# Moving the gate halves of tile 0 forward between the attention heads of a decoder block

## What is computed

```python
h = _modulate(x, sh1, sc1)
z = h @ w_in[l]
q, k, v, gu, gv, ga, gg = jnp.split(z, IN_SPLITS, axis=-1)
attn = _moba_attention(q.reshape(hs), k.reshape(hs), v.reshape(hs))
sgu = _chunked_sgu(gu, gv, sgu_ln_g[l], sgu_ln_b[l], w_spatial[l], b_spatial[l])
merged = (jax.nn.sigmoid(ga) * (attn @ w_attn_up[l])
          + jax.nn.sigmoid(gg) * (sgu @ w_gmlp_up[l]))
out = merged @ w_out[l]
```

## Time and profile before

| what | value |
|---|---|
| time, median of 3 runs | 951.78 us (950.54 to 952.5) |
| the profiled execution: its time | 948.68 us |
| the profiled execution: its span, first to last instruction | 946.9 us |
| PE matmul, busy | 782.7 us, 83% |
| DVE, busy | 605.0 us, 64% |
| ACT, busy | 192.6 us, 20% |
| POOL, busy | 537.0 us, 57% |
| transfers | 340.61 MB, 360 GB/s over the span |
| mean granted clock of PE | 0.923 of full speed |

### The profile page before, as it was taken

How to read it: one execution, slowest core, us unless ns; L and a number is a source line. 1 busy time by engine, 2 the same in 40 slices (tenths; PEclk the granted TensorE clock), 3 DMA queues, 4 the chain that set the end, 5 groups by cost and what they waited for, 6 DMA issues and landing times.

```text
span 946.9 us, 8889 instructions
## 1 busy us (share of the span) xinstructions
PE 782.7 (83%) x2974; PEld 464.0 (49%) x2974; DVE 605.0 (64%) x1359; ACT 192.6 (20%) x485; POOL 537.0 (57%) x529
## 2 busy tenths in 40 slices
PE   5989989999989867786969797797979769596964
PEld 5875568969944423442525353353534335252421
DVE  6356773244586538777674858567585858748556
ACT  1011033202031202231321212132121213312111
POOL 1000000001877776777777777777777777777772
PEclk9999979999999987988979898998989899797988
DMA  9999993323999999999999999999999999999994
GB/s 348 370 371 374 385 384 132 142 81 114 315 402 381 395 397 410 373 371 360 399 409 409 409 409 407 410 408 407 409 403 406 409 409 398 353 404 410 409 410 197
DMA packets 113356, 340.61 MB, mean 360 GB/s; under 512 B 9232, under 2 KB 21024, under 8 KB 113184
## 3 DMA queue, kind: packets, MB, share of 16 engines
q0 software_dynamic: 73728, 268.47, 72.3%
q1 hardware_dynamic: 37008, 69.21, 20.1%
q10 hardware_dynamic: 2576, 2.37, 0.8%
HBM read 338.96 MB, written 1.05 MB: 359 GB/s over the span
## 4 chain that ended last, share of the span: by engine, by line
POOL 35%; PE 29%; DMA 15%; issue 11%; DVE 8%; ACT 1%; SPq 0%; DVEq 0%; POOLq 0%
POOL ring L385 35%; PE bank L1212 13%; DMA ring<-in_w_cond_dram 8%; PE bank L1038 6%; DMA ring<-in_peer_u_dram,small 5%; DVE ln L646 4%; PE bank L1165 3%; PE bank L1187 2%; DMA wpq<-in_w_peer_q_dram 2%; PE bank L1126 2%; PE bank L1135 2%; DVE ring L868 1%; DVE ln L641 0%; PE bank L1087 0%; ACT small L554 0%
## 5 line engine op out<-in xcount | busy, mean ns | idle before, releaser
L1212 PE MATMUL bank<-ring,small 128*128 128x512 f32 x1012 | 474.7, 627 | 134.1 <-ACT small L554 134.1
L868 DVE CUSTOM_DVE_ANT_0 ring<-ring,h_sb 128x1024 f32<-128x1024 f32 x256 | 312.2, 1225 | 190.0 <-DMA ring<-in_peer_u_dram,small 182.7
L385 POOL DMA_INDIRECT ring<-in_peer_u_dram,small x256 | 264.4, 1033 | 263.6 <-DVE small L849 185.8
L1212 PEld LDWEIGHTS bank<-ring,small 128*128 128x128 f32 x1012 | 200.5, 202 | 388.3 <-issue 384.1
L385 POOL DMA_INDIRECT ring<-in_peer_v_dram,small x256 | 268.7, 1050 | 86.0 <-issue 72.9
L554 ACT ACTIVATE small<-ident,small 128x128 f32<-128x128 f32 x253 | 77.3, 388 | 48.4 <-DVE small L861 48.1
L544 ACT ACTIVATE small<-small 128x8 f32<-128x8 f32 x32 | 6.7, 210 | 378.4 <-DVE small L868 378.4
L1187 PEld LDWEIGHTS bank<-hT,wpq 128*128 128x128 f32 x512 | 59.4, 192 | 8.6 <-issue 6.2
L1187 PE MATMUL bank<-hT,wpq 128*128 128x128 f32 x512 | 60.0, 275 | 1.3 <-ACT hT L455 1.2
L646 DVE SCALAR_TENSOR_TENSOR ln<-ring,c_col,ln 128x512 f32<-128x512 f32 x77 | 57.9, 752 | 2.7
L1038 PEld LDWEIGHTS bank<-hT,ring 128*128 128x128 f32 x384 | 46.2, 201 | 2.8 <-issue 2.8
(11 more groups left out here) (158 smaller groups left out, 553.7 us busy)
## 6 DMA issues: line engine op xcount, KB each, us to landing
ring<-in_w_cond_dram SPq DMA_DIRECT2D x10, 2048.0 KB, 11.4
ring<-in_w_in_dram SPq DMA_DIRECT2D x8, 2048.0 KB, 15.2
wpq<-in_w_peer_q_dram SPq DMA_DIRECT2D x8, 1024.0 KB, 19.1
ring<-in_w_cond_dram SPq DMA_DIRECT2D x4, 1024.0 KB, 14.5
wpq<-in_w_out_dram SPq DMA_DIRECT2D x2, 2048.0 KB, 11.6
ring<-in_peer_u_dram,small POOLq DMA_INDIRECT x256, 6.7
ring<-in_peer_v_dram,small POOLq DMA_INDIRECT x256, 6.6
ring<-in_w_in_dram SPq DMA_DIRECT2D x2, 1024.0 KB, 13.5
```

What stands on the lines that cost most here:

```text
L385: nc.gpsimd.indirect_dma_start(out=dst[e], out_offset=None, in_=table[0], in_offset=bass.IndirectOffsetOnAxis(ap=idx[:, k:k + 1], axis=0)) ...
L868: V.tensor_tensor_reduce(u_ring[e], u_ring[e], h_sb[:, n // (2 * HEADS), :], 1.0, 0.0, ALU.mult, ALU.add, acol[:, n % 2, e:e + 1]).then_in ...
L1212: last = T.matmul(bank[ACC_BANKS[t][m]][:], diag[:, e, :], v_ring[e][:, m * BLK:(m + 1) * BLK], start=first, stop=end, skip_group_check=True)
```

## The change

A table says which halves stand behind which head's scores: 0, 1 and 2 behind head 0, half 3 behind head 1, none behind heads 2 and 3, and halves 4 to 7 behind heads 4 to 7 as before. On ACT the saves of halves 0 and 1 move ahead of the square root, the save of half 2 stands behind the exponentials of head 0, and that of half 3 behind those of head 1. Blank lines at the head of the file are dropped too, so the line numbers of the changed program are lower by 17 at ACT's first lines and by 14 on PE.

```diff
+HALVES = ((0, 1, 2), (3,), (), (), (4,), (5,), (6,), (7,))
...
                 if n == 5:
                     for m in range(2, 6):
                         save_wT(m)
+            save_half(0)
+            save_half(1)
             act.wait_ge(gvar_ready, 1)
             nc.scalar.activation(gst[:, 2, :], gst[:, 1, :], ACT.Sqrt, bias=eps[:], scale=1.0 / HD).then_inc(gstd_ready, 1)
...
                                              accum_out=asum[:, 0, j, t:t + 1]).then_inc(exp_done, 1)
-                    save_half(j)
+                    for i in HALVES[j][2 if j == 0 else 0:]:
+                        save_half(i)
...
             for j in range(HEADS + 2):
                 if j < HEADS:
                     scores(j)
-                    gate_half(j)
+                    for i in HALVES[j]:
+                        gate_half(i)
                 if j == 1:
                     cond_total(11)
```

## The result

The changed kernel takes 946.86 us (median of 15 runs, 944.22 to 951.86), the kernel before, beside it, 953.04 us (15 runs, 948.01 to 957.59). The ratio is 0.9944 with a 95% interval of 0.9919 to 0.9968, which on 952 us is 5.3 us less, between 3.0 and 7.7. Forecast were 945.5 us, a range of 943.4 to 949.2, and a gain of 6.3. Most of the 1.4 us between 945.5 and 946.86 is the base: the forecast took 6.3 off the median of three runs of the kernel before, 951.78, and its fifteen runs beside the changed kernel have a median of 953.04. By these medians the gain is 6.2 us, by the ratio 5.3.

What follows compares the result with a forecast made beforehand. A front part on PE and DVE, then a transfer-bound gather tail that starts when it is ready. 4.43 idle plus some 3.8 low clock less 1.9 new idle gives 6.3; 951.78 − 6.3 = 945.5 us, range 943.4 to 949.2.

Steps and rivals of the forecast that it cites:

- The gap and the clock: PE at head 0's turn: 4.43 us of idle time goes, plus some 3.8 us of work at the low clock.
- The new gaps: PE at the turns of heads 1 and 2: new idle time of 0.7 and 1.2 us, 1.9 in all.
- the sum: PE up to half 4: it starts at 144.6 instead of 150.86, a gain of 6.3 us.
- The late square root: ACT ahead of the spatial gate: square root waits for half 1, its save and a table load; DVE continues 2.55 us later.
- the rival of a drain: ACT stands still between last save and table load, priced at 1.28 us; gain 5.0, time 946.8; chance 0.10.
- hidden by 0.55 us: Head 0's turn: probabilities are there at 136.85, PE comes at 137.4, so the late square root costs nothing there.
- The clock in the new gaps: PE at the turns of heads 1 and 2: no clock loss taken; a low clock for a stretch costs 4.5 us, chance 0.09.
- SyncE's queue: Loads behind the total of block 11 go out 7.5 us later, hidden by the attention, at no cost.
- the swallowed case: Tail of gathers: they end at a time their start doesn't set, so 951.8 us would stay; chance 0.08.

Runs made afterwards that it cites:

- filled gap: Kernel before, with five products that nobody reads put on PE behind the total of block 11, nothing else moved; ratio 0.9983 (0.9958 to 1.0009).
- square root first: Changed kernel, with the square root on ACT back ahead of the saves of halves 0 and 1; ratio 0.9938 (0.9908 to 0.9967).
- total early: Changed kernel, with the total of block 11 right behind half 1 on PE instead of behind half 3; ratio 0.9964 (0.9933 to 0.9995).
- ACT alone: Kernel before, with the saves of halves 0 and 1 ahead of the square root and PE's order left alone; ratio 1.0035 (1.0009 to 1.0060).
- changed, third: Changed kernel, unchanged, timed again on one chip beside a variant with halves 4 and 5 moved; ratio 0.9958 (0.9931 to 0.9985), median 947.77 us.
- half 4 early: Changed kernel, with half 4 behind the scores of head 2 instead of head 4; ratio 0.9937 (0.9909 to 0.9966).
- empty heads apart: Changed kernel, with half 4 behind head 2 and half 5 behind head 4, so heads 3 and 5 have none; ratio 0.9904 (0.9873 to 0.9935).
- empty heads apart, again: Same kernel, halves 4 and 5 behind heads 2 and 4, timed again beside the changed kernel; ratio 0.9909 (0.9875 to 0.9944), median 945.41 us.

## Why the prediction was right

**The gap and the clock.** It said that the 4.43 us of idle time and the low clock behind it go. Both did: the turn of head 0 has no wait, the clock is 1.00 through the attention in all three profiles of the changed kernel, and the filled gap shows the clock's share by itself, 3.75 us from the turn of head 0 on (forecast 3.8). 4.43 and 3.75 less the 2.09 of new gaps make 6.1 of the 6.26; of the rest 0.15 is the listing of the gap: from the start of the total to that of the turn it is 4.58 us less than before (136.12 − 135.25 against 134.30 − 128.85).

**The new gaps.** Forecast 0.7 and 1.2 us, measured 1.10 and 0.99, 2.09 instead of 1.9 in sum. The first is longer because PE came to it sooner: three halves behind each other took 10.91 us (119.82 to 130.73), where the sum had three times 3.77. Half 4 came 6.25 us earlier, forecast 6.3.

**The late square root.** Forecast 2.55 us. Counted from the scores of head 0 the reciprocal comes 2.41 later than before (10.33 against 7.92); counted from DVE's own start it is 1.98 (129.30 − 127.63, and 0.31 by which DVE started earlier here). The load is 1.28 us, starts 0.02 after the save and has the square root 0.01 behind it, so the rival of a drain is out. Only the trace says so: the measured time, 946.86 us, is the 946.8 that this rival was priced at. The Trainium skill (ScalarE: Activation LUTs, What ACT_TABLE_LOAD costs) states about 1380 ns of drain for such a switch; these rows differ from it, and the measurement decides. The saves needed no table of their own behind the Gelu: no load stands between the last Gelu (118.22) and the save at 123.69. The delay was hidden at the turn of head 0, but hardly: "hidden by 0.55 us" came out as 0.15. From DVE's division (L735, now L721) to the turn it was 0.60 before (133.70 to 134.30); now the division starts at 135.37, so the turn could have come at 135.97, and PE came at 136.12. For the next two heads the delay was not free, and the sum had it inside the gaps without saying so: DVE works from head 0's start (133.25) to head 2's probabilities (141.68) with no other waits than ACT's exponentials, so PE's gaps at the turns of heads 1 and 2 are DVE's lateness. With the square root first one of the two gaps goes, for a wait of half 2.

**The clock in the new gaps.** No fall, in the three profiles of the changed kernel and in the one with the total early, which has the same two gaps. But the rows that I took as evidence, PE idle around 260 to 264 with the clock staying, were one draw, as the last section shows. The choice was right, its ground was weaker than it looked, and four executions don't tell how much of it was luck.

**SyncE's queue.** Costed at nothing; 106.75 against 106.74 us.

**The tail.** The price of the swallowed case was the whole gain. The timings speak against it. By the ratios, each with an interval of 2.3 to 3.3 us to either side:

| kernel | gain of the front part | gain of the time |
|---|---|---|
| ACT alone | −3.16 | −3.3 |
| filled gap | 2.57 | 1.6 |
| changed | 6.26 | 5.3 |
| changed, third | 6.24 | 4.0 |
| total early | 6.25 | 3.4 |
| square root first | 7.03 | 5.9 |
| half 4 early | 7.35 | 6.0 |
| empty heads apart | 8.48 | 9.1 |
| empty heads apart, again | 8.48 | 8.7 |

Each time agrees with its front part within its interval, and the tail swallows nothing like the whole. But seven of the nine fall short, by 0.1 to 2.9 us, so a loss of about 1 us behind the first gather is not excluded. A front part is read from one execution, and that of the kernel before moved by 0.71 us between two. Where the forecast was off is the single execution: 948.68 − 6.3 = 942.4 against a profiled 946.86. The profiled tail of before was the shortest of the twelve, which the 3.1 us between that execution and the median had already said.

## What to carry to other kernels

A gap in which the matrix engine waits for a late neighbour can cost nearly as much again in the clock behind it: 4.43 us of idle time and 3.75 of clock here. Moving work that was ready into it was worth 6.3 us up to the first gather, with 2.09 us lost again in the emptied heads. When work is taken from later steps to fill an early gap, leave the emptied steps apart from each other: one emptied head was covered by the lead that DVE won next to it; of two in a row the second waited 0.7 us, and where DVE had won no lead yet, in the changed kernel, both waited about 1 us. A stage with a tail that differs by several us from run to run is judged by its own timeline, counted from a common event, and the time only confirms it over many runs.

## What was not expected of the hardware

The same gap did or did not bring the low clock. Ahead of the first sum of rows PE stands still for 3.06 or 3.07 us (3.12 once) in every profile. In the changed kernel's first profile the clock fell soon after the products behind the gap had begun, in its second it did not (PE's timeline of the first, with the granted clock there, then of the second):

```profile
256.32 15.67 PE L1199 MATMUL bank<-ring,small 128*128 128x512 f32 x32 [3.06 <-ACT small L540]
```

```profile
258.00:260.00 2.00, 2.00 (x4) 0.95 (x3) 1.40 (x4) 1.50 (x2) 1.70 (x2) 0.50 1.05 408
```

```profile
258.08 13.97 PE L1199 MATMUL bank<-ring,small 128*128 128x512 f32 x32 [3.06 <-ACT small L540]
```

The 32 rows took 15.67 us in the first and 13.97 in the second. Over the twelve profiles five have 13.97 and seven 15.67 to 16.90. This is one of the things in which tails differ: by 1.7 to 2.9 us of PE's time. How much of it reaches the end isn't shown: the five have tails of 714.2 to 720.0 us, the seven of 715.4 to 727.7.

A shorter gap preceded a fall too. In the second profile of before, half 0 waits 1.49 us for its weights (PE's timeline, then the granted clock):

```profile
123.54 5.46 PE L1038 MATMUL bank<-hT,ring 128*128 128x128 f32 x32 [1.49 <-DMA ring<-in_w_in_dram]
...
136.99 0.69 PE L1087 MATMUL bank<-ident,wpq 128*128 128x128 f32 x3 [2.50 <-DVE wpq L735]
...
139.19 6.16 PE L1038 MATMUL bank<-hT,ring 128*128 128x128 f32 x32
```

```profile
122.00:124.00 2.00, 0.51 (x3) 0.46 (x3) 1.93 (x3) 0.28 (x1) 0.00 (x0) 0.90 1.03 402
124.00:126.00 2.00, 2.00 (x11) 2.00 (x11) 1.97 (x4) 0.00 (x0) 0.00 (x0) 0.50 0.71 212
```

Half 0 takes 5.46 us, and behind the 2.50 us at the turn of head 0 the clock fell a second time, so that half 2 takes 6.16. With the filled gap PE had waited 1.36 us at the same place, and the clock stayed there at 1.00. So the two gaps of about 1 us in the changed kernel, harmless in three profiles, are no proof that such gaps always are; the version without any gap doesn't depend on it.
